# One kernel's first twenty microseconds rearranged: whole token tile and whole first chunk on two DMA queues, and another order of the first products

## The reference, cut to what matters

```python
def _mixer_ab(h, w_in, q_norm, ...):
    proj = jnp.einsum('bsd,df->bsf', h, w_in)          # 256 x 1024 times 1024 x 1440
    c_q, c_kv, k_r, q_s, k_s, v_s = _split_cols(proj, AB_SPLITS)
    q = ... _rms_norm(c_q, q_norm) @ w_uq ...
    # latent attention, sliding-window attention, then the output product

def second_block(x, mem, ...):
    mem_n = rms_norm(mem, mem_norm_g)                  # used by the cross-attention, made early in the kernel
    ...
```

## Time and profile before

| What | Value |
| --- | --- |
| Median of three runs | 916.93 us (916.92 to 916.98) |
| Span of the profiled execution, first to last instruction | 915.3 us |
| Around the span, to the median of the runs | 1.6 us |
| TensorE busy | 907.1 us, 99% of the span |
| VectorE busy | 610.7 us, 67% |
| ScalarE busy | 508.4 us, 56% |
| Mean granted TensorE clock | 0.999 |
| Chain of work that ended last | TensorE 97%, DMA 2%, ScalarE 1% |

### The profile page before, as it was taken

How to read it: one execution, slowest core, us unless ns; L and a number is a source line. 1 busy time by engine, 2 the same in 40 slices (tenths; PEclk the granted TensorE clock), 3 DMA queues, 4 the chain that set the end, 5 groups by cost and what they waited for, 6 DMA issues and landing times.

```text
span 915.3 us, 12823 instructions
## 1 busy us (share of the span) xinstructions
PE 907.1 (99%) x4764; PEld 764.0 (83%) x4764; DVE 610.7 (67%) x1004; ACT 508.4 (56%) x819; POOL 38.2 (4%) x50
## 2 busy tenths in 40 slices
PE   8999999999999999999999999999999999999997
PEld 7888788888888898878888888887888888888886
DVE  4897697776663756769776666376656577574665
ACT  5786555555552456666555555255557564655444
POOL 0100000450000001000000000001000000000000
PEclk9999999999999999999999999999999999999999
DMA  8854436677573577453855557354664565545551
GB/s 297 291 191 129 166 121 230 211 226 251 187 244 117 120 219 235 138 172 128 285 177 187 194 189 248 119 183 145 188 204 137 161 197 163 171 155 186 197 171 72
DMA packets 73036, 169.39 MB, mean 185 GB/s; under 512 B 11336, under 2 KB 33504, under 8 KB 72336
## 3 DMA queue, kind: packets, MB, share of 16 engines
q1 hardware_dynamic: 70512, 157.73, 53.3%
q0 software_dynamic: 2320, 10.58, 3.4%
q10 hardware_dynamic: 144, 0.26, 0.1%
HBM read 167.49 MB, written 1.06 MB: 184 GB/s over the span
## 4 chain that ended last, share of the span: by engine, by line
PE 97%; DMA 2%; ACT 1%; DVE 0%; SPq 0%; issue 0%; DVEq 0%; ACTq 0%
PE psum L789 21%; PE psum L976 15%; PE psum L695 8%; PE psum L697 8%; PE psum L700 8%; PE psum L980 7%; PE psum L1009 7%; PE psum L1014 3%; PE psum L900 3%; PE psum L910 3%; PE psum L904 3%; PE psum L1111 2%; PE psum L672 1%; PE psum L1142 1%; PE psum L1125 1%; DMA arena<-in_mem 1%
## 5 line engine op out<-in xcount | busy, mean ns | idle before, releaser
L1700 DVE TENSOR_TENSOR base_lo<-stage,base_hi 128x1024 fp32r<-128x1024 f32 (+3 forms) x222 | 262.0, 1205 | 95.1 <-ACT base_hi L1299 94.1
L1299 ACT CAST base_hi<-stage 128x1024 fp32r<-128x1024 f32 (+3 forms) x222 | 223.9, 1035 | 52.4 <-PE psum L700 22.5
L1700 DVE TENSOR_TENSOR extra_lo<-stage,extra_hi 128x1024 fp32r<-128x1024 f32 (+1 forms) x68 | 81.1, 1217 | 46.8 <-ACT extra_hi L1299 46.7
L695 PE MATMUL psum<-base_hi,xt 128*128 128x512 f32 (+2 forms) x256 | 100.7, 393 | 0.0
L697 PE MATMUL psum<-base_lo,xt 128*128 128x512 f32 (+2 forms) x256 | 98.3, 384 | 0.4 <-DVE base_lo L1700 0.4
L700 PE MATMUL psum<-base_hi,xt 128*128 128x512 f32 (+2 forms) x256 | 98.4, 385 | 0.0
L1299 ACT CAST extra_hi<-stage 128x1024 fp32r<-128x1024 f32 (+1 forms) x68 | 68.3, 1030 | 49.2 <-PE psum L789 31.6
L789 PE MATMUL psum<-base_hi,ht 128*128 128x512 f32 x288 | 87.3, 393 | 0.0
L976 PE MATMUL psum<-xt,extra_hi 128*128 128x512 f32 x320 | 87.3, 394 | 0.0
L1009 PE MATMUL psum<-xt,base_hi 128*128 128x512 f32 x240 | 76.5, 403 | 0.0
L976 PE MATMUL psum<-xt,base_hi 128*128 128x512 f32 x256 | 69.7, 394 | 0.0
(11 more groups left out here) (244 smaller groups left out, 1572.4 us busy)
## 6 DMA issues: line engine op xcount, KB each, us to landing
stage<-in_w_up SPq DMA_DIRECT2D x80, 512.0 KB, 4.4
stage<-in_w_down SPq DMA_DIRECT2D x44, 512.0 KB, 4.5
stage<-in_w_in_a SPq DMA_DIRECT2D x22, 512.0 KB, 5.2
stage<-in_w_cd_in SPq DMA_DIRECT2D x16, 512.0 KB, 4.6
stage<-in_w_in_b SPq DMA_DIRECT2D x12, 512.0 KB, 3.7
stage<-in_w_ab_in SPq DMA_DIRECT2D x11, 480.0 KB, 6.5
ln_par<-in_ln POOLq DMA_DIRECT2D x4, 1024.0 KB, 7.7
stage<-in_w_ab_out SPq DMA_DIRECT2D x8, 512.0 KB, 3.6
```

The costliest lines, as they stand in the source:

```text
L695: pe.matmul(acc, ah, wh, start=(k == 0), stop=False)
L1299: act.copy(w_hi(c, 0, w), stage_of(c, w)).then_inc(hi_done, 1)
L1700: dve.tensor_tensor(w_lo(c, 0, w), stage_of(c, w), w_hi(c, 0, w).bitcast(F32), ALU.subtract).then_inc(lo_done, 1)
```

## The change

- Loads: tile 0 comes whole (512 KB) as SyncE's first transfer. Chunk 0 comes whole (480 KB), and ScalarE issues it as its own first instruction, on its own queue. SyncE goes on with chunk 1, tile 1 whole, chunk 2, chunk 3, and from there as before.
- The identity matrix is no longer loaded: GpSimd makes it with a memset and two `affine_select`.
- TensorE runs eight matmuls on ones, waits for the identity, turns tile 0's left part, runs one more, and starts. Tile 0's products of k = 0 to 3 come first, with the other three parts turned between them; then tile 1's products of k = 0 to 3, then both tiles' for 4 to 7.
- Chunks 0 and 1 are split in halves. The first half of chunk 0 is rounded by VectorE; ScalarE rounds the other three; VectorE makes the four low halves.
- On ScalarE, chunk 6's high half now comes ahead of `memory_norm`.

```diff
-            load_left(0)
-            sp.dma_start(ident[:, :], d["ident"]).then_inc(loaded["ident"], 16)
+            load_tokens(0)
...
                     if g.c0 + n:
                         load_chunk(g, n)
-                    else:
-                        for m, landed in enumerate((first_staged, staged[STAGE[0]])):
...
                     if g.c0 + n == 1:
-                        load_right()
+                        load_tokens(1)
...
+            pool.memset(ident[:, :], 1.0).then_inc(ident_set, 1)
+            for n, step in enumerate((-1, 1)):
+                pool.wait_ge(ident_set, n + 1)
+                pool.affine_select(out=ident[:, :], in_=ident[:, :], compare_op=ALU.is_ge, fill=0.0, base=0,
+                                   pattern=[[step, P]], channel_multiplier=-step).then_inc(ident_set, 1)
...
+                high([0], xt_hi, turn_hi, [0])
+                low([0], [0])
+                high([1], xt_hi, turn_hi, [0])
+                high([0, 1], xt_lo, turn_lo, [0])
+                low([1], [0])
+                turn_tokens(1)
+                high([2], xt_hi, turn_hi, [0])
+                high([2], xt_lo, turn_lo, [0])
+                turn_tokens(2)
+                high([3], xt_hi, turn_hi, [0])
+                high([3], xt_lo, turn_lo, [0])
+                low([2], [0])
+                turn_tokens(3)
+                low([3], [0])
+                high(range(4), xt_hi, turn_hi, [1])
+                high(range(4), xt_lo, turn_lo, [1])
+                low(range(4), [1])
+                for ks in ((4, 5), (6, 7)):
+                    high(ks, xt_hi, turn_hi, range(TT))
+                    high(ks, xt_lo, turn_lo, range(TT))
+                    low(ks, range(TT))
...
-            ones_by_ones(6)
-            pe.wait_ge(loaded["ident"], 16)
...
+            ones_by_ones(8)
+            pe.wait_ge(ident_set, 3)
+            turn_tokens(0)
+            ones_by_ones(1)
...
+            act.dma_start(stage_of(0, WIDTH[0]), d["w_ab_in"][0]).then_inc(staged[STAGE[0]], 16)
             act.preload_act_table(ACT.Sqrt)
...
+            turn_part(left0, "x0")
+            split_half(0, 1, hi_done)
+            split_half(1, 0, second_hi)
+            split_half(1, 1, hi_done)
+            done["chunks"] = 2
+            turn_part(right0, "x0")
+            turn_part(left1, "x0")
+            split_to(3)
+            turn_part(right1, "x0")
             split_to(NS)
...
-                 ahead_of={3: lambda: [memory_norm(), split_to(done["due"])]})
+                 ahead_of={3: lambda: [split_to(done["due"]), memory_norm()]})
...
+            hi, full = half(0, 0)
+            dve.wait_ge(staged[STAGE[0]], 16)
+            dve.tensor_copy(hi, full).then_inc(first_hi, 1)
+            split_half(0, 0, (first_hi, 1), first_lo)
+            turn_part(left0, xt_hi, xt_lo, 0, "x0")
+            split_half(0, 1, (hi_done, 1), lo_done)
+            split_half(1, 0, (second_hi, 1), first_lo)
+            split_half(1, 1, (hi_done, 2), lo_done)
+            done["chunks"] = 2
+            turn_part(right0, xt_hi, xt_lo, 0, "x0")
+            turn_part(left1, xt_hi, xt_lo, 0, "x0")
+            split_to(3)
+            turn_part(right1, xt_hi, xt_lo, 0, "x0")
             split_to(NS)
```

More of the change, by code:

```diff
@@ L318, in build_program @@
         QK_BANK, LOGIT_BANK, PT_BANK, O_BANK = 4, 5, 6, 7
-        token_parts = [(2 * q + t, t, 4 * q, 4) for q in range(2) for t in range(TT)]
         def row(src, n):
@@ L336, in build_program @@
         hi_done, lo_done = sem("hi_done"), sem("lo_done")
[L337 removed]
+        first_hi, second_hi, first_lo = sem("first_hi"), sem("second_hi"), sem("first_lo")
         chunk_used = sem("chunk_used")
@@ L360, in build_program @@
         constants_set = sem("constants_set")
-        ones_set = sem("ones_set")
+        ones_set, ident_set = sem("ones_set"), sem("ident_set")
         mla_ready, moba_ready = sem("mla_ready"), sem("moba_ready")
@@ L517, in _, with load_tokens @@
         def _(sp):
[L519 to L524, removed]
+            def load_tokens(t):
+                sp.dma_start(x[:, t, :], d["x"][t * P:(t + 1) * P, :]).then_inc(loaded[f"x{t}"], 16)
             def load_memory():
@@ L708, in gemm, with token_step @@
                     step(g, j, hi, lo, k0, turned_by, between)
-            def token_step(name, turn_right):
+            def token_step(name, turn_name, turn_tokens):
                 g = PRODUCTS[name]
[L714 to L743, removed]
-                    for k in ks:
-                        high(k, xt_hi, turn_hi)
-                    if ks[0] == 2:
-                        turn_right()
-                    for k in ks:
-                        high(k, xt_lo, turn_lo)
-                    for k in ks:
-                        low(k)
@@ new lines, in high @@
+                def high(ks, src, made, tiles):
+                    for k in ks:
+                        c, kk = g.c0 + k // g.kp, k % g.kp
+                        pe.wait_ge(*({0: (first_hi, 1), 2: (second_hi, 1)}.get(k) or (hi_done, c + 1)))
+                        for t in tiles:
+                            pe.wait_ge(made, turned_at(turn_name, t, k))
+                            pe.matmul(psum[:, 2 * (g.u0 % 2) + t, 0:g.n], src[:, k, t * P:(t + 1) * P],
+                                      w_hi(c, kk * g.n, g.n), start=(k == 0 and made is turn_hi), stop=False)
@@ new lines, in low @@
+                def low(ks, tiles):
+                    for k in ks:
+                        c, kk = g.c0 + k // g.kp, k % g.kp
+                        pe.wait_ge(*((first_lo, k // g.kp + 1) if k in (0, 2) else (lo_done, c + 1)))
+                        for t in tiles:
+                            last = pe.matmul(psum[:, 2 * (g.u0 % 2) + t, 0:g.n], xt_hi[:, k, t * P:(t + 1) * P],
+                                             w_lo(c, kk * g.n, g.n), start=False, stop=(k == g.kc - 1))
+                        if kk == g.kp - 1 and 1 in tiles:
+                            last.then_inc(chunk_used, 1)
@@ L1173, in _, with turn_tokens @@
             pe.wait_ge(ones_set, 1)
-            ones_by_ones(6)
-            pe.wait_ge(loaded["ident"], 16)
[L1177 to L1183, removed]
+            def turn_tokens(n):
+                part = turn_parts("x0", range(TT))[n]
+                turn_part(part, "x0", tile_of(x), [(loaded[f"x{part[1]}"], 16)])
+            ones_by_ones(8)
+            pe.wait_ge(ident_set, 3)
+            turn_tokens(0)
+            ones_by_ones(1)
             def heads_banks(name):
@@ L1192, in turn_queries @@
                 turn("cq", tile_of(proj0), [(rms_done, 4)])
-            token_step("ab_in", turn_right)
+            token_step("ab_in", "x0", turn_tokens)
             gemm("ab_in", xt_hi, xt_lo, 0, None,
@@ L1507, in down, with split_half @@
                 wide(f"down{layer}", {1: lambda: turn_hidden(layer, 10)}, TAIL)
+            act.dma_start(stage_of(0, WIDTH[0]), d["w_ab_in"][0]).then_inc(staged[STAGE[0]], 16)
             act.preload_act_table(ACT.Sqrt)
[L1511 to L1520, removed]
+            left0, right0, left1, right1 = turn_parts("x0", range(TT))
+            def split_half(c, m, made):
+                act.wait_ge(staged[STAGE[c]], 16 * STAGE_USE[c])
+                act.copy(w_hi(c, m * FIRST, FIRST), stage_of(c, WIDTH[c])[:, m * FIRST:(m + 1) * FIRST]
+                         ).then_inc(made, 1)
+            turn_part(left0, "x0")
[7 more added lines that the diff above has]
+            turn_part(right1, "x0")
             split_to(NS)
@@ L2026, in _, with half, split_half @@
             dve.memset(eps[:, 1:2], RMS_EPS).then_inc(constants_set, 1)
[L2028 to L2043, removed]
+            left0, right0, left1, right1 = turn_parts("x0", range(TT))
+            def half(c, m):
+                return w_hi(c, m * FIRST, FIRST), stage_of(c, WIDTH[c])[:, m * FIRST:(m + 1) * FIRST]
+            def split_half(c, m, ready, made):
+                hi, full = half(c, m)
+                dve.wait_ge(*ready)
+                dve.tensor_tensor(w_lo(c, m * FIRST, FIRST), full, hi.bitcast(F32), ALU.subtract).then_inc(made, 1)
+            hi, full = half(0, 0)
[11 more added lines that the diff above has]
+            turn_part(right1, xt_hi, xt_lo, 0, "x0")
             split_to(NS)
```

6 lines of the change are left out of this document (1 added, 5 removed).

## The result

The changed kernel takes 918.23 us as the median of 20 runs (916.97 to 919.78), the kernel before 916.88 in the same 20 (915.99 to 918.50). The ratio is 1.0013, 95% interval 1.0007 to 1.0019: slower by 0.13%, some 1.2 us (1.35 between the medians), inside the 0.2% that I called no change, and inside the range. The forecast was +0.5.

A forecast was written before the change was run, and what follows sets the result against it. TensorE, busy 907.1 of 915.3 us, was taken to bound the kernel. The larger of two bounds, +0.35 from the start and +0.45 from chunk 6's landing, gave +0.5 on 916.93: 917.4 us, range 916.2 to 918.9.

The forecast's parts named there:

- What can matter: Whole kernel: TensorE never waits after 25.4 us, so whatever shift its queue has by then goes through to the end.
- The landing L: Kernel start: when tile 0 and chunk 0, 992 KB on two queues, have landed; taken as 6.9 us, bounds 5.9 and 7.7.
- L = 7.7: Rival at the kernel start: two queues bring nothing and the old pace stays; +1.15, 918.1 us, chance 0.20.
- Step 0 from L: Step 0: first product at L + 1.43, step 1 at L + 13.5 = 20.4 us against 19.48, 0.9 later.
- The clock: Rival in step 0: TensorE idle until L, so 480-column matmuls run at 1.2 GHz; +2.35, 919.3 us, chance 0.12.
- Chunk 6 first: ScalarE at chunk 6: the new order takes away TensorE's 0.56 us stall, leaving 0.9 - 0.56 = +0.35.
- What is late next: Chunks 7 and 8: ScalarE idles for chunk 6, so chunk 8's low half comes late; TensorE 0.85 or 0.45 us later.
- The sum: Whole kernel: the larger of two bounds, max(L - 6.55, chunk 6's landing - 21.05), 0.35 against 0.45, so +0.5.
- the second bound: Chunks 6 to 8: shift of chunk 6's landing - 21.05, with landing at 21.5 giving +0.45.
- signs of being wrong: Profile after: among them L outside 5.9 to 7.7, products at 0.4 us spacing, and new waits after 32 us.

The follow-up runs named there:

- after_again: The changed kernel once more, unedited: 917.88 us, ratio 1.0009 to the kernel before.
- ident_before: The kernel before with only one edit, GpSimd making the identity matrix instead of loading it: 916.26 us, ratio 0.9993 to the kernel before.
- more_ones: The changed kernel with ten matmul pairs on ones instead of eight before tile 0's transposes and two instead of one behind: 917.27 us, ratio 1.0007 to the kernel before.
- unswap_after: The changed kernel with ScalarE's old order, the memory norm ahead of chunk 6's high half: 917.86 us, ratio 1.0004 to the kernel before.
- swap_before: The kernel before with only chunk 6's high half moved ahead of the memory norm on ScalarE: 917.65 us, ratio 1.0010 to the kernel before.
- fewer_ones_before: The kernel before without the three matmul pairs on ones between turning the two left parts: 917.72 us, ratio 1.0012 to the kernel before.

## Why the prediction was right, and where not

- **What can matter.** Right: one number, the lead or lateness of TensorE's queue by 31 us (+0.79), is nearly the change of the span (+0.64). No wait came after 32 us.
- **The landing L.** Too late: tile 0 at 5.6 and chunk 0 at 5.8 (6.0 and 6.2 in after_again), where I took 6.9 and 5.9 at the least. I drew my line through 7.2 and 9.1, an old pace that had the load of the identity in it, to which I gave no price; ident_before shows that without it tile 1's half lands at 5.6. The rule of "DMA: Bandwidth & Descriptors" in the Trainium skill, section "Issuing engines are not separate DMA queues", agrees with the traces in what it says: chunk 0 landed at 5.8 to 6.2 on two queues, 5.4 to 5.7 on one, and tile 1, issued 0.47 us sooner with two, landed at 8.2 to 8.6 against 8.8 to 9.0. My inference from it, L = 7.7, was wrong, since the old pace was not a matter of queues.
- **Step 0 from L.** I said 1.43 to the first product and 13.5 to step 1; it was 2.0 and 15.4 from tile 0's landing. With the clock up, in more_ones, it was 1.5 and 13.6. So the working of the terms was right to 0.2, but for the clock. VectorE's copy of half a chunk took 0.41 (bound: 0.65), the identity was ready at 1.7 (bound: 3.2).
- **The clock.** This is the step that failed: the sum takes step 0's 48 matmuls at 0.217 us from the first on, and the low clock stood as a rival with 0.12. It is what happens in the changed kernel, to a different degree in each execution. Its size was about right: 2.0 by the rival, 1.58 between two profiles, 1.5 between the medians of the one-queue kernels with and without ones. I held the gap of "nearly 2 us" to be shorter than what the end of the kernel shows and gave it little chance; gaps of 0.8 were enough. The page "TensorE: Matmul & The Clock Gate" of the Trainium skill, section "HAM oscillation", was on the side of the rival: waiting for DMA brings half rate. Its case is a fall from the upper level in waits longer than any here. What the runs show is something else: the clock had not risen yet, and where it had (before, 0.96 us idle at 6.3 to 7.2) it did not fall.
- **Chunk 6 first.** The stall of 0.56 is gone, as said; but unswap_after shows that the order had no part in it.
- **What is late next.** Chunk 6 landed at 19.4, not at 21.5, so the second bound did not bind in the changed kernel. As a mechanism it was right, in swap_before: +0.43 to the attention products for the +0.3 of this reasoning.
- **The sum.** Step 1 was forecast for 20.4 and started at 20.96: L was 1.3 earlier than I took it, and the way from there 1.9 longer (15.4 for 13.5), 1.6 of it the clock. Two of the prediction's signs of being wrong came, L below 5.9 and products 0.4 apart. Two errors stood against each other, and the forecast of +0.5 came closer to +1.2 than its reasons deserved; the range held the time, but the range was built from cases of which I had called the true one unlikely.

What is left open: why the identity's small load delays what is queued behind it by up to 1.9 us, more than its issue and its bytes account for; what picks the moment at which the clock rises; what makes half of swap_before's loss; and how much of the spread of the kernel before (915.9 to 919.3 over all its runs) is the same chance, which I only suppose. Of the 1.35 us between the medians the two profiled spans show 0.64, since the profiled execution of the kernel before was some 0.5 slower than its median one. The prediction's 1.6 us around the span came of that too: over all executions the time less the span is 2.0 us for the kernel before, as for fewer_ones_before and swap_before, which load the identity, and 2.2 in the changed kernel and in all with GpSimd's identity; that 0.2 was not looked into.

## What to carry to other kernels

Until the clock has risen TensorE should not stand idle, also not for a microsecond: put in what computes nothing until the data are there, and count how long it lasts at the slow level and at what moment the landing comes, early or late. Issue first, on one queue, what is needed first; with a second queue the two first transfers land together, and the one that could have come sooner doesn't, though later ones gain. And where a gain doesn't come, look at the distance between the starts of like instructions, not only at waits and busy shares.

## What the runs showed of the hardware

In fourteen profiles, gaps of 0.8 to 1.8 us in TensorE's work in the first 7 us, before the clock had risen, went with a pace of 1.2 GHz until 9.9 to 12.5 us, and gaps of 0.34 or less with a rise at 4.0 to 7.0. Four gaps of 0.5 to 1.0 behind the rise left it up. The granted clock in the windows reads 1.00 from the start of each profile, and the traces' first record of it begins only at the rise, so early in a kernel the spacing must show it. One 64 KB load in 512-byte rows at the head of the queue went with 162 to 181 GB/s in the first 6.1 us (three kernels), and 187 to 189 without it (two). And identical beginnings differed by 0.4 to 0.8 us in the landing of the same transfer from execution to execution (tile 0 at 5.6 and 6.0; tile 1's left half at 7.2, 6.8 and 6.4 in three kernels with the same transfers).
